# Five norms whose six square blocks GpSimd adds up, a memory norm on token rows, a rearranged opening, and two moved orders

## The reference

```python
def rmsnorm(x, g):
    xf = x.astype(jnp.float32)
    y = xf * lax.rsqrt(jnp.mean(xf * xf, axis=-1, keepdims=True) + EPS)
    return (y * g.astype(jnp.float32)).astype(x.dtype)
# layer 1: x = x + mixer(rmsnorm(x, norm_mix_g));  x = x + xattn(rmsnorm(x, norm_x_g), rmsnorm(mem, norm_mem_g))
#          x = x + moe(rmsnorm(x, norm_ffn_g))
# layer 2: NSA, MLP (m0), differential attention (d), MLP (m1), each behind a norm with a scale and shift
```

## Time and profile before

| what | value |
|---|---|
| median of 3 runs | 1316.54 us (1315.47 to 1316.83) |
| profiled execution: its time, its span | 1315.27 us, 1313.5 us |
| granted TensorE clock, mean | 0.998 |
| busy: PE, DVE, ACT, POOL | 1290.3, 950.7, 657.9, 88.5 us (98, 72, 50, 7%) |
| read from HBM | 257.03 MB, 196 GB/s over the span |

### The profile page before, as it was taken

How to read it: one execution, slowest core, us unless ns; L and a number is a source line. 1 busy time by engine, 2 the same in 40 slices (tenths; PEclk the granted TensorE clock), 3 DMA queues, 4 the chain that set the end, 5 groups by cost and what they waited for, 6 DMA issues and landing times.

```text
span 1313.5 us, 24511 instructions
## 1 busy us (share of the span) xinstructions
PE 1290.3 (98%) x10581; PEld 1237.9 (94%) x10581; DVE 950.7 (72%) x1199; ACT 657.9 (50%) x872; POOL 88.5 (7%) x134
## 2 busy tenths in 40 slices
...
GB/s 280 202 206 176 182 176 166 187 135 179 161 288 297 258 258 267 284 284 166 209 128 92 6 161 225 322 313 325 312 235 168 165 97 65 161 192 193 180 174 33
DMA packets 172701, 259.67 MB, mean 198 GB/s; under 512 B 5157, under 2 KB 147794, under 8 KB 172594
## 3 DMA queue, kind: packets, MB, share of 16 engines
...
q10 hardware_dynamic: 840, 1.28, 0.3%
...
HBM read 257.03 MB, written 1.05 MB: 196 GB/s over the span
## 4 chain that ended last, share of the span: by engine, by line
PE 86%; DVE 8%; ACT 3%; issue 2%; DMA 1%; SPq 0%; POOL 0%; ACTq 0%; DVEq 0%
PE ring L675 59%; PE acc L675 24%; ACT w_hi L1503 2%; DVE w_lo L2051 2%; PE acc L1276 1%; DVE arena L2100 1%; PE ring L1085 1%; DMA raw<-in_w_in_dram 1%; ACT h_hi L1503 1%; ACT arena L1503 1%; DMA arena<-in_w_ada_dram 1%; DVE arena L2464 0%; DVE h_lo L2096 0%; DVE h_lo L2094 0%; DVE norm L2066 0%
## 5 line engine op out<-in xcount | busy, mean ns | idle before, releaser
L675 PE MATMUL ring<-h_hi,w_hi 128*128 128x256 f32 (+1 forms) x2016 | 575.0, 285 | 5.7 <-DVE w_lo L2051 1.8
L675 PE MATMUL ring<-h_hi,w_lo 128*128 128x256 f32 (+1 forms) x2016 | 568.2, 282 | 0.0
L675 PE MATMUL ring<-h_lo,w_hi 128*128 128x256 f32 (+1 forms) x2016 | 566.5, 281 | 0.0
L2051 DVE TENSOR_TENSOR w_lo<-raw,w_hi 128x2048 fp32r<-128x2048 f32 x189 | 430.9, 2286 | 165.4 <-ACT w_hi L1503 164.7
L1503 ACT ACTIVATE w_hi<-raw 128x2048 fp32r<-128x2048 f32 x191 | 363.2, 1905 | 132.1 <-PE ring L675 64.0
L675 PEld LDWEIGHTS ring<-h_hi,w_hi 128*128 128x128 f32 x2016 | 379.8, 188 | 11.8 <-issue 7.3
L675 PEld LDWEIGHTS ring<-h_lo,w_hi 128*128 128x128 f32 x2016 | 380.7, 189 | 2.6 <-issue 2.2
L675 PEld LDWEIGHTS ring<-h_hi,w_lo 128*128 128x128 f32 x2016 | 380.9, 189 | 0.0
L675 PE MATMUL acc<-e_hi,w_hi 128*128 128x256 f32 x768 | 216.9, 282 | 2.9 <-DVE e_lo L2752 1.5
L675 PE MATMUL acc<-e_hi,w_lo 128*128 128x256 f32 x768 | 215.1, 280 | 0.0
L675 PE MATMUL acc<-e_lo,w_hi 128*128 128x256 f32 x768 | 215.1, 280 | 0.0
...
## 6 DMA issues: line engine op xcount, KB each, us to landing
...
raw<-in_w_mlp_in_dram SPq DMA_DIRECT2D x32, 1024.0 KB, 5.8
raw<-in_w_mlp_out_dram SPq DMA_DIRECT2D x32, 1024.0 KB, 5.0
raw<-in_w_in_dram SPq DMA_DIRECT2D x24, 1024.0 KB, 5.8
raw<-in_w_e_gate_dram SPq DMA_DIRECT2D x16, 1024.0 KB, 6.3
raw<-in_w_e_up_dram SPq DMA_DIRECT2D x16, 1024.0 KB, 5.4
raw<-in_w_e_down_dram SPq DMA_DIRECT2D x16, 1024.0 KB, 5.0
raw<-in_diff_w_in_dram SPq DMA_DIRECT2D x12, 1024.0 KB, 5.3
```

The source lines that it names most:

```text
L675: return nc.tensor.matmul(dst, lhs, rhs, start=start, stop=stop, **kw)
L2051: tt(w_lo[q % RAW][:, 0:n], raw[q % RAW][:, 0:n], w_hi[q % SPL][:, 0:n].bitcast(F32), ALU.subtract)\
```

## The change

Part by part, with the diff cut to its core:

- **Sums at five norms.** `stat_pair` goes. POOL adds square blocks 2, 3 to 0, 1 once two pairs are squared (`fold_two`, 128x512), then 4, 5 to them once three are (`fold_rest`, 128x512), then block 1 to block 0 (128x256). PE multiplies ones with the one folded block and with blocks 6 and 7 (`stat_sums`), all in `raw_first`, behind block 3, at *d* behind block 6. The folds stand in POOL's list ahead of the gate table's load (*x*), behind the ada load n=1 (*ffn*), behind the ada load n=3 and behind the four first loads (*m0*), behind all ada loads (*d*), behind POOL's two `w_lo` (*m1*).
- **Memory norm.** Row sums by ACT (`accum_out`) on the token rows, root, DVE reciprocal, two row scalings, then the transposes; the gain goes into the copy from PSUM. PE's eight sums, ACT's four squares, DVE's reciprocal and eight scalings at the old place go.
- **Opening.** The first norm's gain has its own semaphore and transpose; `w_lo` of panel 0 moves behind the first two scalings; SP loads panel 2 ahead of the memory rows; panel 1's high and low parts are made in two column halves, each of which PE can start on (`two_halves`).
- **Two orders.** MoE head: ACT and DVE make panel `moe+1+4`'s parts first; ada step 1 stands behind the gating. First MLP: `chunk_lo(1)` ahead of ada step 4.

Several per-norm semaphores are also shared under common names.

```diff
+            def fold_two(tag):
+                pool.wait_ge(*sig(tag + "_squared", 2))
+                nc.gpsimd.tensor_tensor(sq[:, 0:2], sq[:, 0:2], sq[:, 2:4], ALU.add).then_inc(S(tag + "_folded"), 1)
+
+            def fold_rest(tag):
+                pool.wait_ge(*sig(tag + "_squared", 3))
+                pool.wait_ge(*sig(tag + "_folded", 1))
+                nc.gpsimd.tensor_tensor(sq[:, 0:2], sq[:, 0:2], sq[:, 4:6], ALU.add).then_inc(S(tag + "_folded"), 1)
+                pool.wait_ge(*sig(tag + "_folded", 2))
+                nc.gpsimd.tensor_tensor(sq[:, 0], sq[:, 0], sq[:, 1], ALU.add).then_inc(S(tag + "_folded"), 1)
+
...
+                    if n == (1, 3)[l]:
+                        fold_two(("ffn", "m0")[l])
+                        if l == 0:
+                            fold_rest("ffn")
+                if l == 1:
+                    fold_rest("m0")
...
+            fold_two("x")
+            fold_rest("x")
...
+            fold_two("d")
+            fold_rest("d")
...
+            fold_two("m1")
+            fold_rest("m1")
...
-                    for j in sums.get(k, ()):
-                        stat_pair(tag, j)
+                    if k == sums:
+                        stat_sums(tag)
...
+            def stat_sums(tag):
+
+                f, sq = FL[tag + "_stat"], blk(SQX, 8)
+                open_fill(f)
+                pe.wait_ge(*sig(tag + "_folded", 3))
+                mm(bank(f)[:, 0:T], ones[:], sq[:, 0], True, False)
+                pe.wait_ge(*sig(tag + "_squared", 4))
+                mm(bank(f)[:, 0:T], ones[:], sq[:, 6], False, False)
+                mm(bank(f)[:, 0:T], ones[:], sq[:, 7], False, True).then_inc(S(tag + "_summed"), 1)
...
-            sp.wait_ge(S("vecs_landed"), 16 * N_VEC_DMA)
+            sp.wait_ge(S("vecs_landed"), 16 * (N_VEC_DMA - 1))
+            load_panel(sp, turn, 2)
...
+            def two_halves(p, f):
+
+                open_fill(f)
+                wh = w_hi[p % SPL][:].rearrange("p (k n) -> p k n", k=KB)
+                wl = w_lo[p % RAW][:].rearrange("p (k n) -> p k n", k=KB)
+                for b in range(2):
+                    if b == 0:
+                        pe.wait_ge(S("first_half_split"), 1)
+                    else:
+                        open_panel(p)
+                    o, c = bank(f)[:, b * T:(b + 1) * T], slice(b * P, (b + 1) * P)
+                    for k in range(KB):
+                        mm(o, wh[:, k, c], h_hi[:, k, :], k == 0, False)
+                        mm(o, wh[:, k, c], h_lo[:, k, :], False, False)
+                        last = mm(o, wl[:, k, c], h_hi[:, k, :], False, k == KB - 1)
+                last.then_inc(S("panel_done"), 1)
...
-            keep_busy(FL["a_gate"], 5)
+            keep_busy(FL["a_gate"], 4)
...
-            keep_busy(FL["a_gate"], 8)
-            full("a_gate", split="mix_ready", together=1)
-            pe.wait_ge(S("mem_landed"), 16)
+            keep_busy(FL["a_gate"], 4)
+            linear_first([PN["a_gate"]], FL["a_gate"], block_ready("mix_ready"))
+            two_halves(PN["a_gate"] + 1, FL["a_gate"] + 1)
+            pe.wait_ge(S("mem_rows"), 2)
             turn_rows(lambda i: acc[i], 2048, "mem_turned")
             full("a_val")
-            stats("mem", lambda k: blk(SQ + k)[:, 0], "mem_squared")
             for name in ("c_x", "c_c", "c_b", "u_pool"):
...
-            ahead(2 - SPL)
+            act.wait_ge(S("raw_landed1"), 16)
+            for b, sem in ((0, "first_half_hi"), (1, "hi_made")):
+                c = slice(b * P, (b + 1) * P)
+                func(w_hi[1][:].rearrange("p (k n) -> p k n", k=KB)[:, :, c], raw[1][:].rearrange("p (k n) -> p k n", k=KB)[:, :, c],
+                     ACT.Copy).then_inc(S(sem), 1)
+            made["hi"] += 1
+            act.wait_ge(S("mix_ready"), KB)
+            act.wait_ge(S("mem_landed"), 16)
+            for t in range(2):
+                last = func(blk(SQ + 4 * t, 4), arena[:, 2048 + t * D:2048 + (t + 1) * D].rearrange("p (b t) -> p b t", b=4),
+                            ACT.Square, accum_out=stat[:, 4 + t:5 + t])
+            last.then_inc(S("mem_squared"), 1)
+            act.wait_ge(S("mem_squared"), 1)
+            func(stat[:, 6:8], stat[:, 4:6], ACT.Sqrt, scale=1.0 / D, bias=eps[:]).then_inc(S("mem_squared"), 1)
             ahead(0)
             for i in range(2):
...
             func(cond[:], vec[:, 0, VEC["cond"]:VEC["cond"] + KB], ACT.Silu).then_inc(S("cond_made"), 1)
+            ahead(PN["moe"] + 1)
...
+            dve.wait_ge(S("mix_gain_turned"), 1)
+            drains(nc.vector.tensor_copy(mix_gain[:], bank(FL["mix_gain"])[:, 0:KB]), FL["mix_gain"])
+            dve.wait_ge(S("mix_spread"), 1)
+            chain.did(nc.vector.tensor_copy(norm[:, 2, :], acc[0][:, 0:T]))
+            drained_wait(dve, FL["x_t"] + 3)
+            drained_wait(dve, FL["mix_gain"])
+            split_norm("mix", lambda b: mix_gain[:, b:b + 1], mid=SQ, row=2, behind_two=lambda: ahead(1 - SPL))
+            for b, sem, split in ((0, "first_half_hi", "first_half_split"), (1, "hi_made", "panel_split")):
+                c = slice(b * P, (b + 1) * P)
+                dve.wait_ge(S(sem), b + 1)
+                tt(w_lo[1][:].rearrange("p (k n) -> p k n", k=KB)[:, :, c], raw[1][:].rearrange("p (k n) -> p k n", k=KB)[:, :, c],
+                   w_hi[1][:].bitcast(F32).rearrange("p (k n) -> p k n", k=KB)[:, :, c], ALU.subtract).then_inc(S(split), 1)
...
+            dve.wait_ge(S("mem_squared"), 2)
+            chain.did(nc.vector.reciprocal(stat[:, 6:8], stat[:, 6:8]))
+            chain.settle()
+            for t in range(2):
+                rows = arena[:, 2048 + t * D:2048 + (t + 1) * D]
+                ts(rows, rows, stat[:, 6 + t:7 + t], None, ALU.mult).then_inc(S("mem_rows"), 1)
             ahead(0)
             for i in range(4):
                 dve.wait_ge(S("mem_turned"), i + 1)
-                nc.vector.tensor_copy(blk(MEM_T, 8)[:, 2 * i:2 * i + 2].rearrange("p b t -> p (b t)"), acc[i][:])\
-                    .then_inc(S("early_steps"), 1)
+                for b in range(2):
+                    last = ts(blk(MEM_T + 2 * i + b)[:, 0], acc[i][:, b * T:(b + 1) * T], vcol("mem_g", 2 * i + b), None, ALU.mult)
+                last.then_inc(S("mem_scaled"), 1)
             dve.wait_ge(S("pads"), 5)
...
+            ahead(PN["moe"] + 1)
             dve.wait_ge(S("cond_made"), 1)
-            for n in range(2):
-                ada(0, n)
+            ada(0, 0)
             row_wait(0)
             drained_wait(dve, up_fill(0))
             row = flat(GATE_ROWS, row_at(0), T).unsqueeze(1).to_broadcast([P, 2, T])
             act0 = hid(2).rearrange("p (b t) -> p b t", b=2)
             tt(act0, act0, row, ALU.mult).then_inc(S("act_made"), 1)
-            ahead(PN["moe"] + 1)
+            ada(0, 1)
             expert_lo(0)
...
+                chunk_lo(1)
                 if l == 0:
                     ada(1, 4)
-                chunk_lo(1)
```

More of the change, by code:

```diff
@@ L242, in fill_plan @@
     first, count, at = {}, {}, 0
-    for name, n in (("x_t", 4), ("a_gate", 2), ("a_val", 2), ("mem_stat", 1),
+    for name, n in (("x_t", 4), ("mix_gain", 1), ("a_gate", 2), ("a_val", 2),
                     ("c_x", 2), ("c_c", 2), ("c_b", 2), ("u_pool", 2), ("gates", 12), ("x_k", 4), ("x_v", 1), ("ln_stat", 1), ("x_v1", 1), ("lv_stat", 1),
@@ L277, in program @@
                   "raw_ready": (KB, ("x", "ffn", "m0", "d", "m1")), "raw_taken": (2, ("m0", "d", "m1")),
-                  "exp": (1, ("group", "expert", "cmp", "lam")), "silu": (1, ("moe", "cmp")),
+                  "exp": (1, ("group", "expert", "cmp", "lam")), "silu": (1, ("moe", "cmp")), "probs": (16, ("n", "d")), "scored": (16, ("n", "d")), "max": (16, ("n", "d")), "o_done": (8, ("n", "d")), "inverse": (1, ("n", "d", "s")),
+                  "folded": (3, ("x", "ffn", "m0", "d", "m1")),
                   "input_used": (KB - 1, ("gates", "x", "ffn", "moe", "m0", "d", "m1"))}
@@ L534, in _ @@
             loads(sp, turn)
-            p = 2
+            p = 3
             while p < len(plan):
@@ L841, in full @@
                                ready if i == 0 else None)
-                    if norm and i:
-                        stat_pair(norm, i - 1)
-                if norm and not raw:
-                    stat_pair(norm, FL_N[name] - 1)
-            def stat_pair(tag, j, src=lambda k: blk(SQX, 8)[:, k]):
-                f = FL[tag + "_stat"]
-                if j == 0:
-                    open_fill(f)
-                pe.wait_ge(*sig(tag + "_squared", j + 1))
-                for k in (2 * j, 2 * j + 1):
-                    last = mm(bank(f)[:, 0:T], ones[:], src(k), k == 0, k == KB - 1)
-                if j == KB // 2 - 1:
-                    last.then_inc(S(tag + "_summed"), 1)
+            def stat_sums(tag):
[6 more added lines that the diff above has]
+                mm(bank(f)[:, 0:T], ones[:], sq[:, 7], False, True).then_inc(S(tag + "_summed"), 1)
```

78 lines of the change are left out of this document (33 added, 45 removed).

## The result

| what | before | after |
|---|---|---|
| median, us (20 runs each) | 1316.11 (1313.86 to 1317.83) | 1319.26 (1315.67 to 1321.28) |
| ratio, 95% interval | | 1.0021 [1.0014, 1.0028] |
| profiled execution: time, span | 1315.27, 1313.5 | 1320.08, 1318.3 |
| granted TensorE clock, mean | 0.998 | 0.993 |
| busy: PE, DVE, POOL | 1290.3, 950.7, 88.5 | 1282.5, 955.2, 108.0 |

What follows compares the result with a forecast made beforehand. PE, busy 98% of the span, was taken as the bound, except at x, m0 and m1, where ACT's last square ends as late. The terms summed to 6.4 us: 1316.54 - 6.4 = 1310.1, range 1303.0 to 1315.3.

Steps and rivals of the forecast that it cites:

- memory sums: Memory norm near 45 us: PE bound, so removing its 16 ones matmuls gains 3.6 us (2.6 to 3.6).
- ffn: Norm ffn: PE bound, 2.26 us of matmuls less a little of the folds, +2.1 us (1.5 to 2.3).
- x: Norm x: highest gain 0.73 where the square ends, but `fold_rest` delays DVE's lows; -0.15 us (-0.8 to +0.7).
- m1: Norm m1: as m0, with 0.35 us of slack on ACT; -1.05 us (-1.5 to 0).
- opening: Kernel start: earlier panels, but nearly all goes into the wait for the memory, landing near 26.9; +0.2 us (-0.7 to +3.1).
- first MLP's order: First MLP: PE's 1.52 us wait goes, but DVE's 0.71 wait for an ada load stays; +0.5 us (0.3 to 1.5).
- d: Norm d: PE bound, 2.26 less some 0.35 us of `fold_two` beside DVE's lows; +1.9 us (1.2 to 2.2).
- m0: Norm m0: `fold_rest` slows DVE's lows, delaying ACT's last square; no PE saving helps; -1.4 us (-2.1 to 0).
- lows of 3.5 to 4 us: Sign of being right at m0: DVE's six lows take 3.5 to 4 us instead of 2.46, PE waiting ahead of `stat_sums`.
- Rival 2: At x, m0, m1, d: whole lock, DVE losing all of POOL's 2.0 us; sum 4.4, 1312.1 us; chance 0.15.
- MoE head: First expert's low part: PE's 1.18 us wait shrinks, ACT's two gate copies late next; +0.7 us (0.2 to 1.0).
- Rival 5: At the norms' folds: POOL starves behind DVE, PE stands at `stat_sums`; slower by over 0.2% from 7.7 us; chance 0.07.

Runs made afterwards that it cites:

- experiment 2: The changed kernel with the first MLP's order as before (ada step 4 ahead of `chunk_lo(1)`): 1314.53 us, ratio 0.9982 to the kernel before.
- experiment 5: The kernel before with the first MLP's new order alone (`chunk_lo(1)`, then ada step 4): 1321.09 us, ratio 1.0036.
- experiment 6: experiment 4 plus `chunk_lo(1)` ahead of ada step 4 and ada step 5 straight behind step 4: 1309.18 us, ratio 0.9947 to the kernel before.
- experiment 12: experiment 4 with norm d summed over blocks 0, 6 and 7 alone, without POOL adds there: 1307.91 us, ratio 0.9936 to the kernel before.
- experiment 7: experiment 4 with POOL's adds and the shortened sums at m0 too: 1311.43 us, ratio 0.9960 to the kernel before.
- experiment 8: experiment 7 with 14 dummy matmuls on PE behind the last panel ahead of m0: 1313.80 us, ratio 0.9977 to the kernel before.
- experiment 9: experiment 7 with 7 dummy matmuls on PE behind the last panel ahead of m0: 1309.63 us, ratio 0.9957 to the kernel before.
- experiment 10: experiment 4 with m0's POOL adds into an unread tile, PE summing all eight blocks: 1311.14 us, ratio 0.9962 to the kernel before.
- experiment 3: The changed kernel with the MoE head's order as before: 1317.39 us, ratio 1.0007 to the kernel before.
- experiment 4: The changed kernel with POOL's adds at x and ffn only; sums at m0, d, m1 and both orders as before: 1309.87 us, ratio 0.9949.
- experiment 1: The changed kernel with opening and memory norm alone, all five sums and both orders as before: 1311.95 us, ratio 0.9969 to the kernel before.

## Why the prediction was wrong

**Right: memory sums, ffn, x, m1.** 3.44, 2.13, -0.1 and -0.96 against 3.6, 2.1, -0.15 and -1.05. They rested on one price of a ones matmul and on asking, at each norm, whether PE or ACT's last square is late. At x DVE's lows lost 1.2 us, close to the 1.4 taken, so the small net was no luck. The *opening* was under-sized: the memory was taken to land near 26.9, and its square started at 25.05; `a_val` before 32 was one of the prediction's own signs of being wrong; the rest of that working (squares, root, scalings, transposes) took the time that was forecast.

**Failed most: the first MLP's order, +0.5 forecast, -4.1 measured.** The step said "that wait stays and takes back most". It took DVE's wait of 0.71 as fixed by a load whose issue stays put relative to all else. But removing PE's 1.52 us wait is itself what lets the next panel load go out ahead of the ada load, and then the ada load takes 7.7 us instead of 4.6. The row that should have warned stood in the trace of before: the two loads were 1.5 us apart, as much as the wait to be removed. Experiments 2, 5 and 6 show it from three sides. The sum had no term for the clock either: of the 5.9 us lost behind the gain of 1.7, 4.23 are PE's wait, and the rest is about half of the 3.5 us at 0.53 (an estimate).

**Failed: d, +1.9 forecast, -0.4 measured.** "PE bound" was read from PE's queue being full. The reciprocal's place was not looked up: it stands behind two `w_lo` on DVE whatever PE does, and the cap was 1.4 (experiment 12). And the adds' price at d, 0.35, counted only `fold_two`; all three adds fell on the lows and cost 1.8.

**Mis-sized: m0, -1.4 forecast, -3.0 measured** (2.2 to 3.0 in four profiles). The mechanism, adds that stretch DVE's lows while the residual behind them is on the path, was right, and so was the price of `fold_rest`: 1.07 + 0.47 = 1.5 us of DVE. The sign that was named, lows of 3.5 to 4 us, did not come (2.93): most of the price fell on the 128x16 instruction ahead of them, and PE waited ahead of the first raw block, not ahead of `stat_sums`. What was missing is `fold_two` beside a `w_lo` (0.2 in experiments 7 to 10; 0.6 in the kernel after, where that `w_lo` took 2.87) and the half clock behind PE's new wait (0.6 in experiment 9 against 7).

The rule cited from the Trainium skill, *SBUF — State Buffer*, section "SBUF: two separate sides", that the loser of the shared port is blocked for the whole instruction, agrees with the records, for long instructions too: a DVE instruction caught by an add ends only behind it (790.60 behind 790.56, 1126.49 behind 1126.46), and an add that starts beside DVE's ada step (at m0, 788.46) ends 2.10 us on instead of 1.28. Rival 2 had this rule right and its price wrong: `fold_rest`, 2.08 us if alone, took 1.54 from DVE at m0, each add 0.2 to 0.3 less than it lasts. Over all of m0's adds, 1.28 + 1.28 + 0.80 us if alone, DVE lost 1.8 in experiment 10, 0.5 us a us, because `fold_two` fell mostly on a gap.

**Failed: the MoE head, +0.7 forecast, -0.9 measured.** The gain of 0.5 came, though the expert's wait stayed at 0.71, above the 0.6 that was named as a sign. Behind it, the moved ada step 1 frees its buffer later, the load of step 3 is issued at 354.64 instead of 350.6 (358.07 before, less the 7.46 that was gained by then), and DVE and PE wait for it at 362.95 and 367.71. Experiment 3 takes both away. The step had named ACT's gate copies as late next, and left out the loads that an ada step issues.

**Not foreseen: the sparse attention, -3.2** in the profile shown. The clock drop there is in the kernel before and in experiment 4 as well, and its length differs from profile to profile; the change touches nothing near it. The mean clock differs between executions of one kernel too. Ten of the kernel after's twenty have 0.992 or 0.993, as the profiled one, and take 1319.4 to 1321.3 us; the ten others have 0.994 to 0.996 and take 1315.7 to 1319.1; the medians of these two groups are 2.7 us apart, against a measured loss of 3.2. Experiment 1's eleven range from 0.995 to 0.999. Whether the clock is lost at this place in each execution, and why it was longest in the kernel after, is open.

**Rivals.** None of the five gave the time for the reason it named. Rival 5, the slower one, had POOL starve: `fold_rest` would have had to take over 7.7 us, and took 2.10 + 0.94 with its start at 788.46, 3.1 in all.
